# First self-attention by head pairs, its bias table turned once and added by VectorE

## The chip, the cores and the metric

One core of one Trainium2 chip runs the kernel. The time is what the device takes for one execution, in microseconds (us). The kernel before takes 2659.75 us, the median of three runs from 2657.06 to 2670.86. Everything is computed in float32. The engines are TensorE (PE in the profile, its weight loads PEld), VectorE (DVE), ScalarE (ACT), GpSimd (POOL) and SyncE (SP, which issues the DMAs of the weights).

## The reference, cut to what matters

A first block on 256 tokens of width 1024 (attention, then a mixture of 16 experts) is followed by blocks of a second model (latent attention, neighbourhood attention, two feed-forward stages). The change lies in the attention of the first block. Its scores have a bias that depends on the distance of key and query alone.

```python
def diff_attention(qa, ka, va, lam, lambda_init, subln_g, bias_a):     # 4 heads, two sides of 64 features each
    ...
    s1 = jnp.einsum('bhqd,bhkd->bhqk', q1, k1).astype(jnp.float32) + bias
    s2 = jnp.einsum('bhqd,bhkd->bhqk', q2, k2).astype(jnp.float32) + bias
    p = jax.nn.softmax(s1, axis=-1) - lam * jax.nn.softmax(s2, axis=-1)
    return jnp.einsum('bhqk,bhkd->bhqd', p.astype(v.dtype), v)
    ...
    o = rms_norm(o, subln_g, SUBLN_EPS) * (1.0 - lambda_init)
```

The dilated attention beside it has 8 heads of 64 features. Its three window patterns are joined into one softmax whose bias holds the logarithm of how many patterns allow a distance. The results of both, side by side (`mix`, 512 columns each), go through `w_out`.

## The kernel before

**Sizes.** 256 tokens are two halves (`NT` = 2) of 128 rows (`P`), 1024 features are eight blocks (`KC`) of 128. Weights stream through a ring of eight slots. SyncE issues the pieces in the order in which they are planned, each as soon as the piece eight before it has been used: `w_in` (8 pieces), `ada_w` (16), `w_out` (3), then the expert weights `w_gate`, `w_up` and `w_down` with the weights of the latent attention between them.

**Ahead of the attention.** `run_p` and `run_pv` (line 316) make queries and keys (`qkT`, features on the partitions) and values (`vv`, tokens on the partitions). The bias table goes through memory and comes back as `window`, 12 tables of 384 columns, one per head; a row of it stands in reversed order of the partitions, so that it has to be multiplied by `flip`, a reversed identity, before it is a bias.

**The attention** is 16 units: four differential heads with two sides each, then eight dilated heads. A unit has 256 queries against 256 keys, one PSUM bank of 512 columns. Class `Attention` (lines 386 to 516) is shared with the latent attentions of later stages. TensorE's order for unit u is: scores of u+1 (line 413), one piece of the `ada_w` product (line 744, eight matmuls of 384 columns into four groups of 32 output partitions), the four transposes of the probabilities of u (line 425), and the product with the values of u-1 (line 439). The scores (`unit1`, line 968) are for each token half a product of 64 rows, queries against keys, and on top of it a product of 128 rows, `flip` against `window`, which adds the bias. DVE takes the row maxima from PSUM (line 475), copies the transposed probabilities (line 502), takes the reciprocals of the sums (line 508), and puts the result into `mix`, scaled (line 491); the second side of a differential head is scaled by minus lambda as well and added to the first (line 489). ScalarE computes the exponentials (line 464) with the sums beside them.

**Behind the attention** the rows of the `ada_w` product leave PSUM (`row_out`, line 1124: rows 0 and 2 on ScalarE, 1 and 3 on DVE), are turned (`run_ada`), the differential half of `mix` is normed on DVE (lines 1222 to 1233), `run_m` turns all eight blocks of `mix` into `hT`, and `run_o` multiplies by `w_out`. Then come norm, router, expert choice (DVE) and the experts.

**Class `PairAttention`** (lines 519 to 630) does the neighbourhood attention near the end of the program, with 512 columns per side. It takes two heads of 64 features together, adds a bias table from SBUF on DVE, negates and takes the maximum in one instruction (line 612), norms the probabilities ahead of the transposes (line 620), turns them (line 558), and multiplies by the values in four groups of 32 output partitions (line 568), so that the result has the features on the partitions. Its tables are turned by `flip` beforehand (line 285, `na_window`).

## Time and profile before

| | us |
|---|---|
| median of three runs | 2659.75 |
| lowest and highest | 2657.06, 2670.86 |
| profiled execution, its own time | 2659.27 |
| its span in the trace | 2657.5 |
| TensorE busy | 2200.3 (83%) |
| DVE busy | 533.1 (20%) |
| ScalarE busy | 244.6 (9%) |

The mean granted clock of TensorE is 0.949 of full speed. The chain of work that ended last is PE for 58% of the span and DMA for 33%. For a change of one stage the shares of the whole span say little: what counts is which engine has no gap in the stage itself, and whether what follows starts when the stage ends or at a time of its own. The stage changed here runs from 112.40 to 200.18 us.

### The profile page before, as it was taken

How to read it: one execution, taken by the hardware profiler on the slowest of the kernel's cores; microseconds unless marked ns; L12 is line 12 of the kernel's file. 1: busy time of each engine (PE TensorE's matmuls, PEld its weight loads, DVE VectorE, ACT ScalarE, POOL GpSimd, SP SyncE). 2: the span in 40 equal slices, each digit the busy share in tenths (PEclk: the TensorE clock that was granted, in tenths of full speed). 3: DMA queues.
4: the chain of work that ended last, by engine and by line, in shares of the span. 5: the costliest groups of instructions: out<-in, count | busy, mean ns of one | idle time of the engine just before them, and what ended most of it. 6: DMA issues, size and time to landing. Idle time of an engine off the chain costs nothing.

```text
span 2657.5 us, 27028 instructions
## 1 busy us (share of the span) xinstructions
PE 2200.3 (83%) x11636; PEld 1134.9 (43%) x11636; DVE 533.1 (20%) x931; ACT 244.6 (9%) x550; POOL 30.0 (1%) x60
## 2 busy tenths in 40 slices
PE   6996978977687788778778655579989999989998
PEld 5553433432233333333333111146556656445665
DVE  0134111223101101110110311123310021063002
ACT  1121200100000000000000000011110020061000
POOL 0000000000000000000000000000000020000000
PEclk9998989989899899999989889989999999999999
DMA  7671599998999999999999999974094431124450
GB/s 269 251 284 69 223 424 409 425 390 362 425 416 420 419 418 417 420 420 412 420 416 405 424 425 425 423 313 179 16 320 147 153 134 64 64 78 134 152 158 32
DMA packets 146333, 781.00 MB, mean 294 GB/s; under 512 B 11156, under 2 KB 66171, under 8 KB 93491
## 3 DMA queue, kind: packets, MB, share of 16 engines
q1 hardware_dynamic: 139880, 769.45, 72.4%
q10 hardware_dynamic: 6346, 9.95, 1.2%
q8 instruction: 88, 1.44, 0.2%
q14 instruction: 19, 0.15, 0.0%
HBM read 778.29 MB, written 1.07 MB: 293 GB/s over the span
## 4 chain that ended last, share of the span: by engine, by line
PE 58%; DMA 33%; DVE 5%; issue 2%; ACT 1%; ACTq 0%; POOL 0%; SPq 0%; POOLq 0%; DVEq 0%
PE ps L285 15%; DMA ring<-in_mlp_w 12%; DMA ring<-in_w_down 10%; PE ps L1958 8%; PE ps L1965 8%; DMA ring<-in_w_gate 7%; PE ps L1721 4%; PE ps L413 4%; PE ps L1590 3%; PE ps L316 3%; PE ps L1562 3%; PE ps L1567 2%; PE ps L1601 2%; PE ps L439 1%; DMA ring<-in_w_up 1%
## 5 line engine op out<-in xcount | busy, mean ns | idle before, releaser
L1562 PE MATMUL ps<-ring,xe 128*32 128x512 f32 x2048 | 297.5, 648 | 138.7 <-DMA ring<-in_w_up 54.2
L1590 PE MATMUL ps<-ring,expert_work 128*32 128x512 f32 x1408 | 226.0, 703 | 31.4 <-DMA ring<-in_w_down 20.1
L1567 PE MATMUL ps<-ring,xe 128*32 128x256 f32 x2048 | 202.8, 464 | 0.0
L1562 PEld LDWEIGHTS ps<-ring,xe 128*32 128x32 f32 x2048 | 57.4, 113 | 256.4 <-issue 90.9
L1567 PEld LDWEIGHTS ps<-ring,xe 128*32 128x32 f32 x2048 | 73.1, 112 | 171.3 <-issue 171.3
L1590 PEld LDWEIGHTS ps<-ring,expert_work 128*32 128x32 f32 x1408 | 60.7, 123 | 188.6 <-issue 126.3
L1576 PE MATMUL ps<-cst,expert_work 128*128 128x128 f32 x96 | 24.9, 430 | 138.5 <-DVE expert_work L1624 138.5
L1721 PE MATMUL ps<-ring,h 128*128 128x512 f32 x256 | 114.1, 598 | 14.3 <-DMA ring<-in_mlp_w 14.3
L1713 PE MATMUL ps<-hT,ring 128*128 128x256 f32 x512 | 114.8, 382 | 11.6 <-DMA ring<-in_mlp_w 11.6
L1958 PE MATMUL ps<-mlp_x_hT,ring 128*128 128x256 f32 x512 | 114.3, 383 | 1.9 <-DVE mlp_x_hT L364 1.9
L1958 PE MATMUL ps<-mlp_n_hT,ring 128*128 128x256 f32 x512 | 112.6, 379 | 1.8 <-DVE mlp_n_hT L364 1.8
L1965 PE MATMUL ps<-ring,mlp_x_h 128*128 128x512 f32 x256 | 111.8, 592 | 0.0
L1965 PE MATMUL ps<-ring,mlp_n_h 128*128 128x512 f32 x256 | 111.8, 592 | 0.0
L1713 PEld LDWEIGHTS ps<-hT,ring 128*128 128x128 f32 x512 | 96.0, 190 | 33.7 <-DMA ring<-in_mlp_w 19.0
L1958 PEld LDWEIGHTS ps<-mlp_x_hT,ring 128*128 128x128 f32 x512 | 98.4, 192 | 20.5 <-issue 7.4
L1958 PEld LDWEIGHTS ps<-mlp_n_hT,ring 128*128 128x128 f32 x512 | 97.2, 190 | 19.9 <-issue 7.3
L285 PE MATMUL ps<-na_hT,ring 128*128 128x256 f32 (+1 forms) x256 | 82.8, 486 | 1.6 <-ACT na_hT L352 1.6
L1576 PEld LDWEIGHTS ps<-cst,expert_work 128*128 128x128 f32 x96 | 18.5, 221 | 148.3 <-DVE expert_work L1624 148.3
L1721 PEld LDWEIGHTS ps<-ring,h 128*128 128x128 f32 x256 | 47.3, 190 | 78.0 <-issue 78.0
L1618 DVE RECIPROCAL expert_work<-expert_work 128x768 f32<-128x768 f32 x16 | 79.2, 4953 | 0.6
L1810 DVE TENSOR_TENSOR h<-h 128x512 f32<-128x512 f32 x16 | 11.1, 692 | 332.7 <-ACT h L1779 332.7
L1616 DVE TENSOR_SCALAR expert_work<-expert_work 128x768 f32<-128x768 f32 x16 | 8.9, 559 | 318.8 <-ACT expert_work L1608 318.8
(376 smaller groups left out, 2137.6 us busy)
## 6 DMA issues: line engine op xcount, KB each, us to landing
ring<-in_w_gate SPq DMA_DIRECT2D x128, 1408.0 KB, 18.8
ring<-in_w_up SPq DMA_DIRECT2D x128, 1408.0 KB, 19.2
ring<-in_w_down SPq DMA_DIRECT2D x112, 1536.0 KB, 23.7
ring<-in_mlp_w SPq DMA_DIRECT2D x96, 1024.0 KB, 9.0
ring<-in_ada_w SPq DMA_DIRECT2D x32, 1536.0 KB, 9.1
ring<-in_w_in SPq DMA_DIRECT2D x8, 1536.0 KB, 21.8
ring<-in_na_w_qkv SPq DMA_DIRECT2D x12, 1024.0 KB, 9.0
ring<-in_w_down SPq DMA_DIRECT2D x16, 512.0 KB, 23.9
```

The costliest lines, as they stand in the source:

```text
L285: last = nc.tensor.matmul(bank[0:rows, lo:hi], lhsT, rhs, start=start, stop=stop)
L316: last = nc.tensor.matmul(self.part(i), lhsT, rhs, start=(k == 0 and i % self.per == 0), stop=(k == depth - 1), skip_group_check=True)
L413: last = nc.tensor.matmul(ps[:, self.bank + u % 2, lo:hi], lhsT, rhs, start=start, stop=stop, skip_group_check=True)
L1562: nc.tensor.matmul(ps[32 * j:32 * j + 32, up, :], xe[:, k, :], w[:, :, 4 * j:4 * j + 4], start=(k == 0), stop=(k == KC - 1))
L1567: last = nc.tensor.matmul(ps[32 * j:32 * j + 32, 2, 256 * up:256 * up + 256], xe[:, k, :], two, start=(k == 0 and not up), stop=(k == KC - ...
L1590: last = nc.tensor.matmul(ps[32 * j:32 * j + 32, 1 + half, :], hgT[:, at:at + 32], w[:, (c - c0) * D + 512 * half:(c - c0) * D + 512 * hal ...
L1601: last = nc.tensor.matmul(ps[:, 2 * t + half, :], gs[:, t * P:(t + 1) * P], ye[:, 512 * half:512 * half + 512], start=True, stop=True)
L1618: nc.vector.reciprocal(eg[:, 0:768], eg[:, 0:768]).then_inc(e_own, 1)
L1713: last = nc.tensor.matmul(ps[:, 3, S * fc:S * fc + S], w1[:, k, fc * P:(fc + 1) * P], buf["hT"][:, k, :], start=(k == 0), stop=(k == KC - 1))
L1721: last = nc.tensor.matmul(ps[:, CB[2 * t + half], :], m_h1[:, g, S * fc + t * P:S * fc + (t + 1) * P], w2[:, fc, 512 * half:512 * half + 512],
L1958: last = nc.tensor.matmul(ps[:, g % 2, S * fc:S * fc + S], w1[:, k, fc * P:(fc + 1) * P], hT[:, k, :], start=(k == 0), stop=(k == KC - 1))
L1965: last = nc.tensor.matmul(ps[:, 4 + 2 * t + half, :], h1[:, g, fc, t * P:(t + 1) * P], w2[:, fc, 512 * half:512 * half + 512], start=False ...
```

## The change

The first attention no longer uses `Attention` but a class of its own, `FirstAttention`, with eight units instead of 16: a unit is a differential head with both sides, or two dilated heads.

- `run_w1` turns the 12 tables ahead of the attention: 12 matmuls of `flip` against `window` (384 columns), whose results go back into `window`, on ScalarE and DVE in turn. The scores no longer hold a product with `flip`.
- The scores of a unit are four products of 64 rows and 256 columns, in banks 0 and 1, the sides on row halves 0 to 63 and 64 to 127 in turn. The scores of the next unit wait until DVE has taken those of this one (`top`).
- DVE adds the table, negates and takes the extremum in one instruction for each side and token half (256 columns), four to a unit. ScalarE's exponential then reads SBUF. DVE scales the probabilities by the reciprocals; the second side of a differential head is scaled by minus lambda and added to the first, so that one set of probabilities is left to be turned.
- A differential unit has four transposes, a dilated one eight (two sets). ScalarE copies them from PSUM (512 columns each); before, DVE did.
- The values of a differential unit are four products of 128 columns. Those of a dilated unit are eight products with 32 weight columns and 256 moving columns, in four groups of output partitions; their result is `hT` itself, so that `run_m` turns four blocks in place of eight.
- Two pieces of the `ada_w` product stand in each unit. All 16 use banks 6 and 7: after the eighth, ScalarE takes rows 0 and 1 out (`between`), and TensorE waits for that ahead of the ninth (`half0_out`). Rows 0 and 1 no longer leave PSUM behind the attention.
- `vrow`, `hot` and `plog` move into other buffers, and lambda into another column. Norms of the differential results are as before.

```diff
+                self.turns, n = [], 0
+                for unit in units:
+                    sides = range(1) if unit["lam"] is not None else range(2)
+                    self.turns.append([n + b for b in sides])
+                    n += len(sides)
...
+            def pe(self, pe):
+                def scores(u):
+                    if u >= 1:
+                        pe.wait_ge(self.top, 4 * u)
+                    q, k = self.units[u]["qk"]
+                    for t in range(NT):
+                        for b in range(2):
+                            rows = slice(HD * b, HD * b + HD)
+                            last = nc.tensor.matmul(ps[:, b, t * S:t * S + S], qkT[rows, q, t * P:(t + 1) * P], qkT[rows, k, :],
+                                                    start=True, stop=True, skip_group_check=True)
+                    last.then_inc(self.scored, 1)
+                def turn_over(u):
+                    for b, i in enumerate(self.turns[u]):
+                        pe.wait_ge(self.scaled, 4 * u + (4 if len(self.turns[u]) == 1 else 2 * b + 2))
+                        if i >= 2:
+                            pe.wait_ge(self.copied, i - 1)
+                        for c in range(2):
+                            for t in range(NT):
+                                at = t * S + c * P
+                                last = nc.tensor.transpose(ps[:, 2 + i % 2, (c * NT + t) * P:(c * NT + t) * P + P],
+                                                           self.probs[u % 3][:, b, at:at + P], ident)
+                        last.then_inc(self.turned, 1)
+                def times_values(u):
+                    pe.wait_ge(self.copied, self.turns[u][-1] + 1)
+                    if u >= 2:
+                        pe.wait_ge(self.out, u - 1)
+                    for out, lhsT, rhs, start, stop in self.units[u]["values"](ps[:, 4 + u % 2, 0:S], self.probsT[u % 2]):
+                        last = nc.tensor.matmul(out, lhsT, rhs, start=start, stop=stop, skip_group_check=True)
+                    last.then_inc(self.valued, 1)
+                n = len(self.units)
+                scores(0)
+                for u in range(n):
+                    self.fill(pe, 2 * u)
+                    if u >= 1:
+                        times_values(u - 1)
+                    if u + 1 < n:
+                        scores(u + 1)
+                    self.fill(pe, 2 * u + 1)
+                    turn_over(u)
+                times_values(n - 1)
...
+            def act(self, act, between):
+                n = len(self.units)
+                for u in range(n + 1):
+                    if u < n:
+                        for b in range(2):
+                            for t in range(NT):
+                                probs = self.probs[u % 3][:, b, t * S:t * S + S]
+                                act.wait_ge(self.top, 4 * u + 2 * b + t + 1)
+                                if u >= 3:
+                                    act.wait_ge(self.inverse, u - 2)
+                                nc.scalar.activation(probs, probs, ACT.Exp, bias=self.columns(0, u, 2 * b + t, 1), scale=-1.0,
+                                                     accum_out=self.columns(1, u, 2 * b + t, 1)).then_inc(self.exped, 1)
+                    if u >= 1:
+                        for b, i in enumerate(self.turns[u - 1]):
+                            act.wait_ge(self.turned, i + 1)
+                            if u >= 3:
+                                act.wait_ge(self.valued, u - 2)
+                            nc.scalar.activation(self.probsT[(u - 1) % 2][:, b, :, :].rearrange("p c q -> p (c q)"),
+                                                 ps[:, 2 + i % 2, :], ACT.Identity).then_inc(self.copied, 1)
+                    between(act, u)
...
+            def dve(self, dve):
+                n = len(self.units)
+                for u in range(n + 1):
+                    if u >= 2:
+                        self.result(dve, u - 2)
+                    if u == n:
+                        continue
+                    unit = self.units[u]
+                    dve.wait_ge(self.scored, u + 1)
+                    if u >= 3:
+                        dve.wait_ge(self.turned, self.turns[u - 3][-1] + 1)
+                    for b in range(2):
+                        for t in range(NT):
+                            nc.vector.tensor_tensor_reduce(self.probs[u % 3][:, b, t * S:t * S + S], ps[:, b, t * S:t * S + S],
+                                                           unit["table"](b, t), -1.0, 0.0, ALU.add, ALU.min,
+                                                           self.columns(0, u, 2 * b + t, 1)).then_inc(self.top, 1)
+                    dve.wait_ge(self.exped, 4 * u + 4)
+                    nc.vector.reciprocal(self.columns(2, u), self.columns(1, u)).then_inc(self.inverse, 1)
+                    dve.wait_ge(self.inverse, u + 1)
+                    if unit["lam"] is not None:
+                        second = self.columns(2, u, 2, 2)
+                        link(dve, nc.vector.tensor_scalar(second, second, unit["lam"], None, ALU.mult))
+                    for b in range(2):
+                        for t in range(NT):
+                            part = self.probs[u % 3][:, b, t * S:t * S + S]
+                            inv = self.columns(2, u, 2 * b + t, 1)
+                            if b and unit["lam"] is not None:
+                                whole = self.probs[u % 3][:, 0, t * S:t * S + S]
+                                dve.wait_ge(self.scaled, 4 * u + t + 1)
+                                last = nc.vector.scalar_tensor_tensor(whole, part, inv, whole, ALU.mult, ALU.add)
+                            else:
+                                last = nc.vector.tensor_scalar(part, part, inv, None, ALU.mult)
+                            last.then_inc(self.scaled, 1)
+                self.result(dve, n - 1)
+            def result(self, dve, u):
+                dve.wait_ge(self.valued, u + 1)
+                self.units[u]["evac"](ps[:, 4 + u % 2, 0:S]).then_inc(self.out, 1)
...
-        def unit1(q, k, hh, table, v, out, minus=None):
-            lo = HD * (hh % 2)
-            sc = []
-            for t in range(NT):
-                sc.append((t * S, t * S + S, qkT[lo:lo + HD, q, t * P:(t + 1) * P], qkT[lo:lo + HD, k, :], True, False))
-                off = P * (1 - t)
-                sc.append((t * S, t * S + S, flip, window[:, table, off:off + S], False, True))
-            return {"nt": NT, "scores": sc, "v": v, "out": out, "minus": minus}
...
+        for hh in range(DIFF_HEADS + DIL_HEADS // 2):
+            diff = hh < DIFF_HEADS
+            qk = (hh, 4 + hh) if diff else (8 + hh - DIFF_HEADS, 12 + hh - DIFF_HEADS)
+            def table(b, t, hh=hh, diff=diff):
+                n = hh if diff else DIFF_HEADS + 2 * (hh - DIFF_HEADS) + b
+                return window[:, n, P * (1 - t):P * (1 - t) + S]
+            def values(bank, turned, hh=hh, diff=diff):
+                if diff:
+                    return [(bank[:, t * P:t * P + P], turned[:, 0, c, t * P:t * P + P], vv[:, c, P * hh:P * hh + P], c == 0, c == 1)
+                            for t in range(NT) for c in range(2)]
+                return [(bank[32 * n:32 * n + 32, :], vv[:, c, P * hh + 32 * n:P * hh + 32 * n + 32], turned[:, n // 2, c, :],
+                         c == 0, c == 1) for c in range(2) for n in range(4)]
+            def evac(bank, hh=hh, diff=diff):
+                if diff:
+                    return nc.vector.tensor_copy(mix[:, :, P * hh:P * hh + P], bank.rearrange("p (t f) -> p t f", t=NT))
+                return nc.vector.tensor_copy(hT[:, hh, :], bank)
+            units.append({"qk": qk, "lam": small[:, 60:61] if diff else None, "table": table, "values": values, "evac": evac})
...
-        att1 = Attention("a1", units, probs, probsT, fill=lambda pe, u: ada_piece(pe, 0, u, ada_base, 4 + 2 * (u // KC)))
+        rows0 = view(vac, 4, ADA_W)
+        def row_out(row, bank, eng):
+            src = ps[:, bank, 0:ADA_W]
+            return nc.scalar.activation(row, src, ACT.Identity) if eng == "act" else nc.vector.tensor_copy(row, src)
+        def fill(pe, i):
+            if i == KC:
+                pe.wait_ge(half0_out, 1)
+            ada_piece(pe, 0, i, ada_base, 6)
+        def between(act, u):
+            if u == KC // 2:
+                act.wait_ge(ada_done.sem, ada_base + KC)
+                row_out(rows0[:, 0, :], 6, "act")
+                row_out(rows0[:, 1, :], 7, "act").then_inc(half0_out, 1)
...
+        run_w1 = Run([Job([((P, 0, WIN), flip, window[:, n, :], True, True, False, None)],
+                          *turn(n, window[:, n, :], cols=WIN)) for n in range(12)], (2, 3, 4, 5))
+        att1 = FirstAttention(units, probs1, probsT1, fill)
         @block.tensor
         def _(pe):
...
             run_pv.finished(pe)
+            run_w1.pe(pe)
+            run_w1.finished(pe)
             att1.pe(pe)
...
-            att1.act(act)
+            run_w1.ev(act, "act")
+            att1.act(act, between)
         @block.vector
         def _(dve):
-            att1.dve(dve, dve_own, dve_count)
+            run_w1.ev(dve, "dve")
+            run_w1.finished(dve)
+            att1.dve(dve)
...
-        run_m = Run(transposes(KC, lambda t, c: mix[:, t, c * P:(c + 1) * P], lambda c: hT[:, c, :],
+        run_m = Run(transposes(DIFF_HEADS, lambda t, c: mix[:, t, c * P:(c + 1) * P], lambda c: hT[:, c, :],
...
-            row_out(rows0[:, 0, :], 4, "act").then_inc(a2.sem, a2("row0"))
...
-            row_out(rows0[:, 1, :], 5, "dve").then_inc(v2.sem, v2("row1"))
...
```

On TensorE, in the attention, a unit stood like this before; it is one side of a differential head (`ps<-qkT` and `ps<-window,cst` are scores, these two rows stand twice, `ps<-ring,scp` is the `ada_w` piece, `ps<-cst,probs` the transposes, `ps<-vv,probsT` the values):

```order
L413 MATMUL ps<-qkT 128x256 [waits exp_done]
L413 MATMUL ps<-window,cst 128x256
...
L744 MATMUL ps<-ring,scp 32x384 [waits slot1_loaded]
L744 MATMUL ps<-ring,scp 32x384 x7
L425 MATMUL ps<-cst,probs 128x128 [waits probT_sb,exp_done]
L425 MATMUL ps<-cst,probs 128x128 x3
L439 MATMUL ps<-vv,probsT 128x128 [waits probT_sb]
L439 MATMUL ps<-vv,probsT 128x128 x3
```

Now a unit is the whole head (this is the third of four); `kTc` and `table_parts` are further buffers of the probabilities and of their transposes:

```order
L871 MATMUL ps<-ring,scp 32x384 [waits slot4_loaded]
L871 MATMUL ps<-ring,scp 32x384 x7
L681 MATMUL ps<-vv,table_parts 128x128 [waits a1_copied]
L681 MATMUL ps<-vv,table_parts 128x128 x3
L660 MATMUL ps<-qkT 128x256 [waits a1_top]
L660 MATMUL ps<-qkT 128x256 x3
L871 MATMUL ps<-ring,scp 32x384 [waits slot5_loaded]
L871 MATMUL ps<-ring,scp 32x384 x7
L672 MATMUL ps<-cst,kTc 128x128 [waits a1_copied,a1_scaled]
L672 MATMUL ps<-cst,kTc 128x128 x3
```

For a head, eight products of scores have become four, eight transposes four, and eight value products four; the two pieces are still two.

On ScalarE, at the end of the attention before, the first rows of the `ada_w` product (`vac`) came last, behind all exponentials:

```order
L464 ACTIVATE probs,small<-ps,small 128x256 [waits out_done,probT_done,max_done]
L464 ACTIVATE probs,small<-ps,small 128x256
L1197 UNCONDITIONAL_BRANCH
L1124 ACTIVATE vac<-ps 128x384 [waits ada_done]
L1124 ACTIVATE vac<-ps 128x384
L1203 ACT_TABLE_LOAD
```

Now rows 0 and 1 stand in the middle of it, between the copies of the transposes of two units:

```order
L706 ACTIVATE kTc,small<-kTc,small 128x256 [waits a1_inverse,a1_top] x4
L713 ACTIVATE table_parts<-ps 128x512 [waits a1_valued,a1_turned]
L1126 ACTIVATE vac<-ps 128x384 [waits ada_done]
L1126 ACTIVATE vac<-ps 128x384
L706 ACTIVATE kTc,small<-kTc,small 128x256 [waits a1_inverse,a1_top] x4
L713 ACTIVATE probsT<-ps 128x512 [waits a1_valued,a1_turned] x2
```

The `vac` rows have moved up, behind the exponentials of the fifth unit and the copy of the fourth, and TensorE's ninth piece waits for them.

## Rows read from the trace of the kernel before

**Rows 1.** Timeline, PE, one unit: start us, us, engine line op tiles xcount [idle].
```profile
124.82 0.70 PE L413 MATMUL ps<-qkT 64*128 64x256 f32 x2
...
127.33 1.50 PE L744 MATMUL ps<-ring,scp 128*32 128x384 f32 x16
128.76 0.66 PE L425 MATMUL ps<-cst,probs 128*128 128x128 f32 x4
129.25 1.06 PE L439 MATMUL ps<-vv,probsT 128*128 128x128 f32 x8
130.24 0.70 PE L413 MATMUL ps<-qkT 64*128 64x256 f32 x2
```

**Rows 2.** Busy time by stretch: PE, PEld, DVE, ACT, POOL; granted clock, DMA share, GB/s.
```profile
108.00:112.00 4.00, 3.52 (x9) 1.26 (x7) 1.13 (x2) 1.20 (x2) 0.00 (x0) 1.00 1.02 433
...
112.40:200.20 87.80, 86.53 (x576) 47.36 (x576) 32.85 (x84) 18.50 (x67) 0.00 (x0) 1.00 0.83 301
200.00:204.00 4.00, 2.55 (x12) 2.42 (x12) 3.80 (x8) 0.07 (x1) 0.00 (x0) 0.62 0.49 210
...
250.00:286.00 36.00, 20.93 (x72) 11.31 (x72) 18.29 (x36) 5.92 (x13) 0.00 (x0) 0.73 0.00 0
...
2320.00:2360.00 40.00, 36.22 (x230) 17.51 (x228) 24.89 (x78) 20.21 (x49) 0.00 (x0) 1.00 0.32 105
```

**Rows 3.** Timeline, PE and DVE, the attention's ends and what follows.
```profile
112.40 0.67 PE L413 MATMUL ps<-qkT 64*128 64x256 f32 x2 [0.88 <-DVE vv L359]
...
199.70 0.48 DVE L491 TENSOR_SCALAR h<-ps,small 128x64 f32<-128x64 f32 x2 [1.26 <-PE ps L439]
200.28 1.02 DVE L1124 COPY vac<-ps 128x384 f32<-128x384 f32 x2
...
206.11 2.18 PE L283 MATMUL ps<-cst,h 128*128 128x128 f32 x16 [1.87 <-DVE modc L761]
...
208.91 27.70 PE L285 MATMUL ps<-ring,hT 128*128 128x512 f32 x64 [0.62 <-ACT hT L352]
```

**Rows 4.** Timeline, PE, the turning of the tables of the neighbourhood attention.
```profile
2173.77 5.34 PE L285 MATMUL ps<-na_window,cst 128*128 128x384 f32 x16
```

**Rows 5.** Timeline, PE, the neighbourhood attention; and line 316's products of 256 columns.
```profile
2342.51 1.05 PE L568 MATMUL ps<-na_hT,na_v 128*32 128x256 f32 x16
2343.49 1.13 PE L547 MATMUL ps<-na_kT,kTc 64*128 64x512 f32 x4
2344.55 1.09 PE L558 MATMUL ps<-cst,na_window 128*128 128x128 f32 x8
...
28.57 55.49 PE L316 MATMUL ps<-hT,ring 128*128 128x256 f32 x256 [0.98 <-DVE plog L829]
```

**Rows 6.** Timeline, DVE, the neighbourhood attention: one unit, 512 columns a side.
```profile
2345.28 0.69 DVE L612 CUSTOM_DVE_ANT_1 na_window<-ps,ring 128x512 f32<-128x512 f32 x1
...
2346.25 0.17 DVE L618 RECIPROCAL small<-small 128x1 f32<-128x1 f32 x1 [0.27 <-ACT na_window L599]
2346.45 0.49 DVE L620 TENSOR_SCALAR na_window<-na_window,small 128x512 f32<-128x512 f32 x1
...
2350.43 0.42 DVE L2293 COPY kTc<-ps 128x256 f32<-128x256 f32 x1
```

**Rows 7.** Timeline, ACT: exponential of 256 columns, row outs, exponential of 512, copies.
```profile
115.71 0.47 ACT L464 ACTIVATE probs<-ps,small 128x256 f32<-128x256 f32 x1 [4.41 <-DVE small L475]
...
196.50 0.87 ACT L1124 ACTIVATE vac<-ps 128x384 f32<-128x384 f32 x2 [2.56 <-PE ps L744]
...
2345.40 0.72 ACT L599 ACTIVATE na_window<-na_window,small 128x512 f32<-128x512 f32 x1 [1.29 <-DVE small L612]
...
2346.82 1.06 ACT L589 ACTIVATE na_hT<-ps 128x512 f32<-128x512 f32 x2
```

**Rows 8.** SyncE's first issue after the attention (timeline); an `ada_w` piece, median us to landing.
```profile
236.65 0.93 SPq L243 DMA_DIRECT2D ring<-in_mla_w_dq  x2
...
ring<-in_ada_w SPq DMA_DIRECT2D x16, 1536.0 KB, 7.6
```

42 lines of the change are left out of this document (22 added, 20 removed).

## Prediction

> **What bounds the kernel now.** I read four views, in this order. The busy time by stretch comes first [rows 2]: in the attention, 112.40 to 200.20 us, TensorE is busy for 86.53 of 87.80 us, at full clock, while DVE has 32.85 and ScalarE 18.50. So the stage costs what TensorE's instructions cost, and only what leaves TensorE there shortens it. The timeline of one unit [rows 1] says what they are: from 124.82 to 130.24 are 5.42 us, of which the scores take 2.51, the `ada_w` piece 1.43, the transposes 0.49 and the values 0.99. 16 units make the stage. The third view is what follows it [rows 3]: the last result leaves DVE at 200.18, and the output projection starts at 208.91. Between them runs one chain on DVE with two bursts of transposes. The fourth is whether the rest waits for this stage or for the memory. SyncE's first issue after the stage is at 236.65 [rows 8], and the DMA share is 0.00 from 250 to 286 [rows 2]: the ring is full and the expert stage starts when its inputs are computed. So a microsecond won in the attention should be a microsecond at the end, although the experts themselves are fed at DMA pace.
>
> **What TensorE pays in the new stage.**
> Turning the tables: eight matmuls of 384 columns took 5.34 us elsewhere [rows 4], about 0.65 each with the overlaps. 12 x 0.65 = 7.8, and 0.6 for the last result to leave PSUM, with nothing beside it on TensorE. From 112.40 that gives 120.8 for the first scores.
> Scores: four products of 256 columns, alternating between the row halves. The pair of 512 columns in the neighbourhood attention starts 1.06 us before the next work [rows 5], where one after the other they would need 4 x 0.43 = 1.7 (55.49 us for 256 instructions, two to a product, is 0.43 for 256 columns [rows 5]). It has the same number of column passes as ours, so 1.06. Bounds: 1.06 and 1.7. 8 x 1.06 = 8.5.
> Pieces: 16 x 1.43 = 22.9, as before.
> Transposes: four sets of 0.49 for the differential heads and eight for the dilated ones, 12 x 0.50 = 6.0.
> Values: a differential unit has the four products that a unit had before, 0.99. A dilated one has eight products in four column groups; the same eight took 0.98 in the neighbourhood attention (2342.51 to 2343.49 [rows 5]), against 8 x 0.43 = 3.4 if they don't overlap. 4 x 0.99 + 4 x 0.95 = 7.8.
> Sum: 8.5 + 22.9 + 6.0 + 7.8 = 45.2 us, or 5.4 for a differential unit and 5.9 for a dilated one.
>
> The Trainium skill, "TensorEngine Tiling (Array Packing)", section Key Properties, says that a change of tiling mode drains TensorE. The trace agrees for the old scores, where 64 rows and 128 rows alternate: 2.51 / 4 = 0.63 for each product [rows 1] against 0.43 where nothing alternates [rows 5]. Read strictly it charges a differential unit one change more than I count, some 0.2, which would make the sum 1.6 worse.
>
> **What DVE and ScalarE pay for a unit.** From the scores on: the first table addition is 256 columns, 0.69 for 512 [rows 6] less the 0.27 by which the 256-column copy (0.42) is shorter, so 0.42. Then four exponentials, 0.47 from PSUM at 256 columns and 0.72 from SBUF at 512 [rows 7]; I take 0.50 each, 2.0. The other three additions hide under them. Then a reciprocal 0.17, the lambda step with its link some 0.27, and four scalings of 256 columns, 0.49 for 512 [rows 6], so 0.28 to 0.42 each, 1.4 together. With the result copy of 0.42 and semaphores that is 4.8 us per unit, against 5.4 to 5.9 on TensorE. ScalarE has 2.0 and one or two copies of 0.53 [rows 7], 3.1 at most. TensorE therefore stays the bound by about 0.6, a thin margin at the start of the stage and in the differential half.
>
> **Waits of TensorE in the new stage.** I followed the queues by these numbers. (1) The start: the first unit has no unit before it whose values could fill the time. The scores of unit 1 wait 0.2 for the additions of unit 0, its transposes 0.5 for the scalings (ready at 126.4), and its values 1.1, because ScalarE's copy stands behind the exponentials of unit 1. After that TensorE is late enough for the others. (2) The ninth piece: ScalarE must finish the exponentials of unit 4, the copy of unit 3 (0.53) and two rows (0.87 [rows 7]). Behind the transposes of unit 3 this makes 2.1; with the exponentials done it would be 1.5. Queued behind it on TensorE are the values of unit 3 and the scores of unit 5. (3) The end: the last values wait 0.75 for the last copy, which no other work covers. Together 1.8 + 2.1 + 0.75 = 4.6 us. Bounds: 2.5 (the start covered, the ninth piece at 1.5) and 8 (0.4 more in each unit).
>
> End of TensorE's part: 120.8 + 45.2 + 4.6 = 170.6; the last copy by DVE ends at 171.0. Before it was 200.18: **29.2 us less**.
>
> **Behind the stage.** Row 1 no longer leaves PSUM on DVE's chain: half of 1.02 [rows 3], 0.5. `run_m` turns four blocks, not eight: half of 2.18 and of the copies that trail it, 1.0 of the 2.80 between 206.11 and 208.91 [rows 3]. ScalarE's row and its table load fit under DVE's squares as before. 1.5 us less.
>
> **Transfers.** At full backlog the DMAs move 433 GB/s [rows 2], 3.6 us for a piece of 1.57 MB. The new stage uses a piece every 2.8 us, but starts with eight in the ring. The ninth is issued when the first is used, at about 123.3, and lands after 7.6 [rows 8], the sixteenth some 7 x 3.66 later, at 156 to 157. It is wanted at about 166. `w_out` follows until about 167, wanted at 178. Covered at no cost; the cover is some 10 us wide.
>
> **Sum.** 29.2 + 1.5 = 30.7 us. The profiled execution took 2659.27, half a microsecond off the median of 2659.75, so 2659.3 - 30.7 = 2628.6; with a small part of the mode changes, **2629**.
>
> **Rivals.**
> (A) *DVE and ScalarE set the pace.* For it: 4.8 against 5.4 is little, every unit has a ring of semaphores through three engines, and no row shows these instructions at 256 columns. If the additions are 0.45, the exponentials 0.60, the scalings 0.40 to 0.50, a unit comes to 5.6 to 5.8 and the stage to 175.0, 2633. If all cost as much as at 512 columns, some 7.5 a unit, 8 x 7.5 = 60: 2644. Against it: the fixed part of each row is small beside its columns. The Trainium skill warns of this in "TensorEngine Tiling (Array Packing)", section PSUM Bottleneck: tiling speeds TensorE but not the evacuation of PSUM, which may become the bottleneck.
> (B) *The small products don't overlap.* Scores 1.7 (+5.1 for eight units) and dilated values 3.4 (+9.9): 2644. Against it stand the 1.06 and 0.98 of the same forms [rows 5].
> (C) *Transfers.* If pieces come no faster than at the pace of 301 GB/s of the old stage [rows 2], 5.2 us each, the sixteenth lands near 168 and `w_out` near 182: +4, 2633. Against it: 433 GB/s in the backlog.
> (D) *Slower than before: the clock.* The granted clock was 0.62 from 200 to 204 [rows 2], behind waits. The new stage has more waits. If TensorE ran at 1.2 instead of 2.4 GHz through it, 45.2 + 7.8 us would double: +53, 2682. It turns slower than before from 31 us, that is 60% of the stage at the low level. Against it: the neighbourhood attention has waits in each unit, 36.22 us busy of 40, and kept 1.00 [rows 2].
> (E) *Nothing arrives at the end.* The stage is shorter, but the experts wait for weights whose transfer ends no earlier: 2659. It decides if their first five pieces land later than the router is done. They are issued from about 157 on and need some 17 us; the experts start near 256.
>
> **How the numbers follow.** Forecast (2625 to 2632) 0.67; A 0.14, B 0.06, C 0.04, D 0.03, E 0.03, and 0.03 for more gain, should the waits vanish. The range is the forecast with its bounds, C and the lighter part of A: 2624 to 2636, 0.8 or a little more. A gain of over 0.5% (13 us, about what a measurement can tell from none) holds in all but D and E: faster 0.94, same 0.03, slower 0.03.
>
> **What would show it.** Right: first scores at 120.8, eight units of 5.4 to 5.9 in TensorE's timeline, one wait of about 2 us ahead of the ninth piece, the last result near 171, the projection near 178, and the expert stage 30 to 31 us earlier, with equal gaps from there on. Wrong: waits of TensorE for DVE's scalings in every unit (A), scores of 1.7 or values of 3.4 (B), waits for `ada_w` or `w_out` (C), a granted clock under 1.00 between 121 and 170 (D), experts that start earlier and then wait longer for the ring (E).

## The result, and the profile after

The changed kernel takes **2630.07 us**, the median of four executions from 2628.27 to 2637.34. The kernel before, run beside it, takes 2662.91 (four executions, 2657.06 to 2670.86). The ratio is 0.9885, with a 95% interval from 0.9864 to 0.9906: faster, by 25 to 36 us. Forecast were 2629 and a gain of 30.7 us, which is a ratio of 0.9885 as well.

The profiled execution is the longest of the four: 2637.34, a span of 2635.5. It is 21.9 us below the profiled execution of before, not 30.7. Most of this text is about the 9 us between these two numbers.

The page of after, busy time of each engine (us, share of the span, instructions):

```profile
PE 2174.7 (83%) x11540; PEld 1120.3 (43%) x11540; DVE 530.0 (20%) x966; ACT 252.8 (10%) x567; POOL 29.9 (1%) x60
```

TensorE has 96 instructions less and is busy for 25.6 us less than before (2200.3 in the table ahead); DVE is about where it was. Now the stage itself, TensorE's timeline (start, us from first to last, engine, line, operation, output and inputs, count; in brackets the idle time ahead of the row and what ended it):

```profile
116.09 7.98 PE L285 MATMUL ps<-window,cst 128*128 128x384 f32 x24 [0.88 <-DVE vv L359]
124.81 1.14 PE L660 MATMUL ps<-qkT 64*128 64x256 f32 x8 [0.74 <-DVE window L359]
...
127.66 1.13 PE L660 MATMUL ps<-qkT 64*128 64x256 f32 x8 [0.28 <-DVE small L730]
...
130.65 0.66 PE L672 MATMUL ps<-cst,probs 128*128 128x128 f32 x4 [0.43 <-DVE probs L746]
...
133.58 1.16 PE L681 MATMUL ps<-vv,probsT 128*128 128x128 f32 x8 [0.85 <-ACT probsT L713]
134.67 1.13 PE L660 MATMUL ps<-qkT 64*128 64x256 f32 x8
...
137.16 0.66 PE L672 MATMUL ps<-cst,kTc 128*128 128x128 f32 x4
137.75 1.50 PE L871 MATMUL ps<-ring,scp 128*32 128x384 f32 x16
139.18 1.16 PE L681 MATMUL ps<-vv,table_parts 128*128 128x128 f32 x8
140.26 1.13 PE L660 MATMUL ps<-qkT 64*128 64x256 f32 x8
...
150.86 2.29 PE L871 MATMUL ps<-ring,scp 128*32 128x384 f32 x16 [1.86 <-ACT vac L1126]
153.08 1.98 PE L681 MATMUL ps<-vv,table_parts 128*128 128x128 f32 x8
154.99 1.13 PE L660 MATMUL ps<-qkT 64*128 64x256 f32 x8
...
158.51 1.50 PE L871 MATMUL ps<-ring,scp 128*32 128x384 f32 x16
159.82 1.05 PE L681 MATMUL ps<-probsT,vv 128*32 128x256 f32 x16
160.80 1.14 PE L660 MATMUL ps<-qkT 64*128 64x256 f32 x8
...
175.53 1.07 PE L681 MATMUL ps<-table_parts,vv 128*32 128x256 f32 x16 [0.74 <-ACT table_parts L713]
177.90 1.50 PE L283 MATMUL ps<-cst,vac 128*128 128x128 f32 x12 [1.30 <-DVE vac L1126]
182.57 1.97 PE L283 MATMUL ps<-cst,h 128*128 128x128 f32 x8 [3.16 <-DVE modc L888]
185.16 29.59 PE L285 MATMUL ps<-ring,hT 128*128 128x512 f32 x64 [0.62 <-ACT hT L352]
```

These rows answer to those of [rows 1] and [rows 3]. From one scores row to the next, 134.67 to 140.26, a differential unit takes 5.59 us, for two sides; [rows 1] had 5.42 for one. A dilated unit takes 5.81, 154.99 to 160.80, for two heads. The brackets are all the waits of the stage: 0.74, 0.28, 0.43 and 0.85 at the start, 1.86 ahead of the ninth piece, 0.74 at the end. All other rows of the stage follow each other without one. The stage ends with the last result's copy at 176.67 + 0.42 = 177.09, so it takes 61.00 us from 116.09, against 87.78 before.

Three of these rows are longer than their neighbours of the same form: the ninth piece has 2.29 where 1.50 is usual, the values behind it 1.98 for 1.16, and the output projection 29.59, where before had 27.70. The stretches of after show TensorE's granted clock there (length; then busy us and instructions of PE, PEld, DVE, ACT and POOL; granted clock, DMA share, GB/s):

```profile
121.00:145.00 24.00, 21.70 (x184) 10.69 (x183) 14.56 (x59) 11.10 (x38) 0.00 (x0) 1.00 0.80 326
152.00:154.00 2.00, 2.00 (x12) 0.92 (x5) 0.00 (x0) 0.00 (x0) 0.00 (x0) 0.50 0.98 418
...
182.00:184.50 2.50, 1.93 (x8) 1.57 (x8) 1.35 (x8) 0.82 (x2) 0.00 (x0) 0.53 1.00 424
184.50:188.00 3.50, 2.88 (x5) 1.32 (x5) 0.48 (x1) 0.12 (x1) 0.00 (x0) 0.50 0.50 207
```

The clock is full (2.4 GHz) until the wait of 1.86, at 1.2 GHz behind it, and again at 1.2 GHz behind the wait of 3.16. Between the two, `run_ada` (177.90) takes 1.50 at full clock. In the profile of before it took nearly twice as long, in the stretch from 200 to 204 us whose granted clock was 0.62 [rows 2]:

```profile
201.45 2.79 PE L283 MATMUL ps<-cst,vac 128*128 128x128 f32 x12 [1.79 <-DVE vac L1124]
```

A third place at a lower pace lies ahead of the change. The first projections (line 316), which no edit touches, took 58.53 us in the profile of after and 55.49 in that of before [rows 5]. TensorE's timeline of after:

```profile
29.23 58.53 PE L316 MATMUL ps<-hT,ring 128*128 128x256 f32 x256 [0.98 <-DVE table_parts L959]
```

Six microseconds of it, columns as in the stretches above:

```profile
29.00:35.00 6.00, 5.77 (x14) 4.64 (x15) 0.00 (x0) 0.00 (x0) 0.00 (x0) 1.00 1.02 421
```

The same six of `e_side_order`, an experiment that differs from after only in the attention:

```profile
29.00:35.00 6.00, 6.00 (x29) 5.30 (x28) 0.00 (x0) 0.00 (x0) 0.00 (x0) 1.00 1.02 425
```

Of the same matmuls 14 fit in where 29 do in the other: half the pace. The column of the granted clock reads 1.00 in both, so here the pace has to be read from the instructions. The matmul ahead of them (line 285, at 26.37) took 1.88 against 1.08 as well. This is why the stage begins at 116.09 and not at 112.40.

**The account of the 8.8 us**, profile against profile (forecast 30.7, seen 21.9):

| | forecast | profile of after | missing |
|---|---|---|---|
| start of the stage | 112.40 | 116.09 | 3.7 |
| stage | 87.8 - 29.2 = 58.6 | 61.0 | 2.4 |
| last result to projection | 7.2 | 185.16 - 177.09 = 8.07 | 0.8 |
| projection | 27.70 | 29.59 | 1.9 |

Of the 2.4 in the stage, 0.8 + 0.8 are the two long rows at 1.2 GHz. Of the 0.8 behind it, all is `run_m`, whose eight transposes took 1.97 where 1.09 is usual. With the start and the projection that makes 8.0 us of half-pace stretches; the other 0.8 us are true errors of the sum, told below.

### The profile page after: what moved, and what is told of

The parts are those of the page before. It is cut to its first block, busy times and chain, and to the rows that moved or that the text cites. A ratio compares the mean times of both kernels' runs of the same rounds, so it can differ in the third digit from the quotient of the medians.

```text
span 2635.5 us, 26842 instructions
## 1 busy us (share of the span) xinstructions
PE 2174.7 (83%) x11540; PEld 1120.3 (43%) x11540; DVE 530.0 (20%) x966; ACT 252.8 (10%) x567; POOL 29.9 (1%) x60
## 4 chain that ended last, share of the span: by engine, by line
PE 59%; DMA 31%; DVE 5%; issue 2%; ACT 2%; SPq 1%; ACTq 0%; POOL 0%; POOLq 0%; DVEq 0%
PE ps L285 16%; DMA ring<-in_mlp_w 10%; DMA ring<-in_w_down 10%; PE ps L2109 8%; PE ps L2116 8%; DMA ring<-in_w_gate 7%; PE ps L1741 4%; PE ps L1872 4%; PE ps L1713 3%; PE ps L316 3%; PE ps L413 2%; PE ps L1718 2%; PE ps L1752 2%; SPq L218 1%; DVE expert_work L1769 1%
## 5 line engine op out<-in xcount | busy, mean ns | idle before, releaser
L1741 PE MATMUL ps<-ring,expert_work 128*32 128x512 f32 x1408 | 225.5, 707 | 30.6 <-DMA ring<-in_w_down 19.4
L1961 DVE TENSOR_TENSOR h<-h 128x512 f32<-128x512 f32 x16 | 11.1, 692 | 332.6 <-ACT h L1930 332.6
## 6 DMA issues: line engine op xcount, KB each, us to landing
ring<-in_w_in SPq DMA_DIRECT2D x8, 1536.0 KB, 21.9
```

The costliest lines, as they stand in the source:

```text
L1741: last = nc.tensor.matmul(ps[32 * j:32 * j + 32, 1 + half, :], hgT[:, at:at + 32], w[:, (c - c0) * D + 512 * half:(c - c0) * D + 512 * hal ...
```

## The experiments

All times "of the stage" are from TensorE's first work after the value projection to the end of the last result's copy. A single execution is uncertain by some 5 us (the four of after span 9), so where a part is judged I read the stage and give the total beside it; the total of a single execution can't resolve a part smaller than that.

### Both kernels again

The changed kernel and the one before, unchanged, to see which of the slow stretches belong to the kernel.

> The changed kernel once more. Theory 1 (the 7 us by which its profiled execution is longer than its other runs are stretches at 1.2 GHz that fall elsewhere in each execution): the profile is 3 to 8 us shorter than 2637.34, the queries and keys projections take 55.5 us in place of 58.5 unless a low stretch falls on them again, and the stage from the first table product to the last result is again 59 to 61 us. Theory 2 (they belong to the new kernel): the same three places (first projection, ninth piece, output projection) are at the low clock again, and the time is 2637.

Median 2630.35 (2625.44 to 2636.44, four executions) against 2659.99 (seven), ratio 0.9885 (0.9859 to 0.9911). TensorE's timeline:

```profile
28.93 58.13 PE L316 MATMUL ps<-hT,ring 128*128 128x256 f32 x256 [0.98 <-DVE table_parts L959]
...
150.17 2.69 PE L871 MATMUL ps<-ring,scp 128*32 128x384 f32 x16 [1.86 <-ACT vac L1126]
...
184.48 29.39 PE L285 MATMUL ps<-ring,hT 128*128 128x512 f32 x64 [0.62 <-ACT hT L352]
```

All the long rows are back, the ninth piece behind the same wait, and the stage is 61.0 us again. One thing differs: here `run_ada` is at the low clock already (2.42 for 1.50), and the wait behind it is 2.24, not 3.16.

> The kernel before once more, for its profile. If the low clock in the output projection belongs to the new kernel, the projection takes 27.7 us again. If it is chance, it takes 29 or more here in one case of two. The 512-column stretch of the queries and keys at the start takes 55.5 or 58 to 58.6 us by chance, as in the others.

2665.74 us. This profile of the old kernel has fast first projections (55.49) but a slow output projection:

```profile
205.94 3.67 PE L283 MATMUL ps<-cst,h 128*128 128x128 f32 x16 [1.87 <-DVE modc L761]
210.24 29.53 PE L285 MATMUL ps<-ring,hT 128*128 128x512 f32 x64 [0.62 <-ACT hT L352]
```

So 29.53 is possible for the old kernel too. My theory that the low clock of the projection belongs to the new kernel alone falls. Over all profiles, those of the new form without filled gaps had 29.3 to 30.6 in nine of nine, those of the old form 27.70, 27.70 and 29.53 (the second is `e_before_no_table`, below). But the granted clock fell to 0.50 behind the stage in all three of the old form as well; what differs is which rows it fell on. In before these were `run_ada`'s alone, in `e_before_no_table` `run_ada` and `run_m` (2.01 and 3.41), in `e_before_again` all three.

The low clock at the ninth piece does not come with every execution. Of eight profiles with a wait of 1.86 to 1.90 ahead of it, only after and `e_after_again` have a long ninth piece; in the other six it takes 1.50. Nor do the slow first projections follow from the change: over 14 profiles they are there in seven (56.9 to 58.6 us), in kernels of both forms, and no edit but that of the table's store reaches ahead of them.

### What the bias product costs

In the kernel before, the product of `flip` and `window` is taken out of the scores. This leaves the bias out.

```
-                sc.append((..., qkT[lo:lo + HD, q, ...], qkT[lo:lo + HD, k, :], True, False))
-                sc.append((..., flip, window[:, table, off:off + S], False, True))
+                sc.append((..., qkT[lo:lo + HD, q, ...], qkT[lo:lo + HD, k, :], True, True))
```

> The kernel before without the products of the table, so the bias is left out of the first attention. Theory (TensorE bounds the old stage by the sum of its instructions, and 64-row and 128-row products in turn cost 0.63 each where they need 0.43): scores go from 2.51 to about 1.06 us a unit, a unit from 5.42 to about 4.0, the stage from 87.8 to about 65 us. If the table product only costs its own 0.43 and hides nothing else, 1.65 us remain for the scores and the stage is 74. Rival (the old stage is bound by the ring of waits through DVE and ScalarE): it stays over 80.

2644.08 us, and the stage falls from 87.8 to 64.0. TensorE's timeline:

```profile
123.41 1.13 PE L413 MATMUL ps<-qkT 64*128 64x256 f32 x4
124.47 1.50 PE L744 MATMUL ps<-ring,scp 128*32 128x384 f32 x16
...
127.37 1.13 PE L413 MATMUL ps<-qkT 64*128 64x256 f32 x4
```

A unit takes 3.96 (123.41 to 127.37; its neighbours 3.97), not 5.42; the scores start 1.06 before the next work, not 2.51. So the two bias products and the changes between 64 and 128 rows cost 1.45 us of each of 16 units, 23 us together, most of what the change wins. The rest of the change, turning the tables included, brings the stage from 64.0 to 59.4 (the next run). A second thing stands in these rows: x4 is two products, both on one half of the rows, and they take the same 1.06 as the four products over both halves in the new kernel. Twice 0.43, the price of a product of 128 rows and 256 columns [rows 5], leaves 0.2 for the changes of form on either side; the other half's products come on top at no cost.

### The order of the row halves

The forecast took 1.06 for the scores because the halves alternate.

```
-                    for t in range(NT):
-                        for b in range(2):
+                    for b in range(2):
+                        for t in range(NT):
```

> The changed kernel with one edit: the four score products of a unit run side by side no longer alternate between the row halves, both products of one half come first. Theory (products on the two halves run at the same time only when they alternate): scores go from 1.06 to 1.3 to 1.7 us a unit, the stage gets 2 to 5 us longer. Rival (each product costs its columns anyway and the saving in the scores is only the missing change of mode): scores stay at 1.06, the stage is the same within 0.5 us.

2631.82 us. TensorE's timeline:

```profile
130.68 1.14 PE L660 MATMUL ps<-qkT 64*128 64x256 f32 x8
131.75 1.50 PE L871 MATMUL ps<-ring,scp 128*32 128x384 f32 x16
...
146.90 1.50 PE L871 MATMUL ps<-ring,scp 128*32 128x384 f32 x16 [1.87 <-ACT vac L1126]
```

Still 1.06, with both products of one half issued ahead of the other's. My reason was wrong, the number right: the halves run side by side, but they needn't alternate for it. This run is also a clean view of the stage. The wait of 1.87 is there and no low clock behind it; the stage takes 112.10 to 171.53, **59.4 us** against 58.6 forecast (`e_gap_filled`, below, has 59.4 too). Its projection still has 29.57.

### How far DVE is from being the bound (rival A)

Copies of 256 columns are added on DVE in each unit, between the reciprocal and the scalings.

```
+                    for _ in range(2):          # the other run: range(6)
+                        link(dve, nc.vector.tensor_copy(extra[:, :], window[:, 0, 0:S]))
```

> The changed kernel with two extra copies of 256 columns on DVE in each unit, between the reciprocals and the scalings, some 0.8 to 1.0 us a unit on the path to the transposes. Theory (TensorE sets the pace and DVE has 0.65 us to spare in a unit): the stage gets 2 to 4 us longer, most of it at the start and in the differential units. Rival A (DVE and ScalarE set the pace already): 8 units by 0.9, 7 us longer or more.

2633.02 us. TensorE's timeline of it:

```profile
130.87 0.66 PE L672 MATMUL ps<-cst,probs 128*128 128x128 f32 x4 [1.08 <-DVE probs L748]
```

DVE's timeline of it, in a differential unit:

```profile
138.87 0.62 DVE L737 COPY extra<-window 128x256 f32<-128x256 f32 x2
...
141.11 0.42 DVE L1120 COPY h<-ps 128x256 f32<-128x256 f32 x1
141.66 0.42 DVE L730 CUSTOM_DVE_ANT_0 probs<-ps,window 128x256 f32<-128x256 f32 x1
```

The two copies add 0.65 us to each unit, less than I had expected, and DVE has almost no gap left: its first addition follows the result copy by 0.13. In DVE's timeline of after the same place has a gap of 0.65:

```profile
140.37 0.42 DVE L1117 COPY h<-ps 128x256 f32<-128x256 f32 x1
141.44 0.43 DVE L730 CUSTOM_DVE_ANT_0 probs<-ps,window 128x256 f32<-128x256 f32 x1 [0.65 <-PE ps L660]
```

TensorE's units stay at 5.59 and 5.81; only the start shows it, where the wait for the scalings grows from 0.43 to 1.08. The stage is 60.0 us, 0.6 more than 59.4, where I had expected 2 to 4.

> The changed kernel with six extra copies on DVE in each unit; two cost DVE 0.65 us, so six cost 1.95. Theory (DVE had 0.65 us to spare in a differential unit of 5.59 and about 1.2 in a dilated one of 5.81): differential units get 1.3 us longer, dilated ones 0.8, the start 1.9; the stage goes from 59.4 to 67 to 70 us. If DVE's true margin is larger, because its wait for ScalarE's exponentials can take some of it, 63 to 65.

2639.48 us. Six copies, 1.95 us, break it: the stage is 67.05, 7.6 more than 59.4. Up to 3.2 us of that are low clock, in two places (2.79 for a piece and 0.97 for the transposes ahead of it at the start, 2.45 and 1.84 for the ninth piece and the values behind it). The rest are waits: 2.40 for the scalings at the start, 0.32 and 1.00 for ScalarE's copy in the next units, which take 5.98 and 6.67, and 3.18 ahead of the ninth piece. TensorE:

```profile
152.43 2.45 PE L873 MATMUL ps<-ring,scp 128*32 128x384 f32 x16 [3.18 <-ACT vac L1129]
```

0.65 us in a unit is hidden and 1.95 is not. That the margin is about what the forecast said (0.6) rests on DVE's gap of 0.65; these two runs only bracket it. Without the low clock the stage would take 63.9 to 65.4 us (an estimate: 67.05 less 3.2, or less the 1.6 at the ninth piece alone), less than the 67 to 70 of the theory.

### The two sides turned apart

The second side of a differential head isn't added to the first; both are turned and multiplied.

```
-                    sides = range(1) if unit["lam"] is not None else range(2)
+                    sides = range(2)
...
-                            if b and unit["lam"] is not None:
-                                ...
-                                last = nc.vector.scalar_tensor_tensor(whole, part, inv, whole, ALU.mult, ALU.add)
-                            else:
-                                last = nc.vector.tensor_scalar(part, part, inv, None, ALU.mult)
+                            last = nc.vector.tensor_scalar(part, part, inv, None, ALU.mult)
...
-                    return [(bank[...], turned[:, 0, c, ...], vv[...], c == 0, c == 1) for t ... for c ...]
+                    return [(bank[...], turned[:, b, c, ...], vv[...], b + c == 0, b + c == 2) for t ... for b ... for c ...]
```

> The changed kernel with the two sides of a differential head turned and multiplied apart, added up in PSUM. Theory (TensorE bound): four more transposes (0.5) and four more value products (1.0) in each of four units, the stage 6 us longer. Rival: TensorE had idle time there, and 3 us or less are lost.

2635.38 us, the stage 64.5, 5.1 more. TensorE:

```profile
136.64 2.05 PE L681 MATMUL ps<-vv,table_parts 128*128 128x128 f32 x16
...
143.56 2.05 PE L681 MATMUL ps<-vv,probsT 128*128 128x128 f32 x16
```

A differential unit takes 6.92 (136.64 to 143.56), not 5.59. Joining the sets is worth 1.33 in each of four units.

### The ninth piece behind the values

The piece that waits for the first two rows of `ada_w` is moved behind the values of unit 3 and the scores of unit 5.

```
-                    self.fill(pe, 2 * u)
+                    if u != n // 2:
+                        self.fill(pe, 2 * u)
...
+                    if u == n // 2:
+                        self.fill(pe, 2 * u)
```

> The changed kernel with the ninth piece of the modulation product behind the values of unit 3 and the scores of unit 5 instead of ahead of them. Theory: the wait of 1.86 us ahead of it goes, and the low clock that followed it in the profile (the piece 2.2 in place of 1.43 us, the values 1.9 in place of 1.1) goes too; the stage is 1.5 to 3.5 us shorter. Rival: the values of unit 3 wait for the same ScalarE queue, and 1 us or less is left of the gain.

2632.67 us, the stage 58.5. That is 0.9 less than 59.4, the rival's figure. It is 2.5 less than the 61.0 of after, but the low clock in that is absent from most profiles anyway. TensorE:

```profile
146.30 1.16 PE L681 MATMUL ps<-vv,table_parts 128*128 128x128 f32 x8 [1.11 <-ACT table_parts L716]
```

The wait of 1.86 becomes one of 1.11, for ScalarE's copy of the transposed set, which the next work needs. ScalarE's queue is what is late here, not the piece.

### The table read in its own order

The turning of the tables is 8.7 us in which TensorE does nothing else. It is needed because a row of `window` starts one element further for each partition. If the store writes a copy of each table for each partition (128 rows of 512 elements per head), a read that steps 511 elements from the last element of the first row delivers the other order, and neither `flip` nor `run_w1` is needed.

```
-        table_dram = nc.dram_tensor("bias_table", [12, 512], F32).ap()
+        table_dram = nc.dram_tensor("bias_table", [12, P, 512], F32).ap()
...
-            sp.dma_start(table_dram, plog[0:12, :])
-            src = bass.AP(..., offset=table_dram.offset, ap=[[1, P], [512, 12], [1, WIN]])
+            sp.dma_start(table_dram, plog[0:12, :]....to_broadcast([12, P, 512]))
+            src = bass.AP(..., offset=table_dram.offset + P - 1, ap=[[511, P], [P * 512, 12], [1, WIN]])
...
-            run_w1.pe(pe)
...
-            run_w1.ev(act, "act")
-            run_w1.ev(dve, "dve")
+            dve.wait_ge(win_loaded, 16)
```

> The changed kernel with the tables turned by the memory instead of TensorE: the table is stored 128 times in a row, and read with a step of 511 from one partition to the next, so that it arrives turned. The 12 table products and their copies are gone. Theory: the first scores start where the first table product started, 8.7 us earlier, and all of it arrives at the end: 8 to 9 us less than the changed kernel. Rival: the larger store and its reading (3 MB each way) run beside the loads of the first weights and hold up the projections or arrive after 112 us: the same time or longer.

**2619.0 us** (2618.77 to 2621.03, four executions) against 2663.81 (seven), ratio 0.9837 (0.982 to 0.9853), an interval clear of the changed kernel's. It beats both kernels. TensorE's timeline:

```profile
112.40 1.14 PE L660 MATMUL ps<-qkT 64*128 64x256 f32 x8 [0.87 <-DVE vv L359]
...
170.25 29.40 PE L285 MATMUL ps<-ring,hT 128*128 128x512 f32 x64 [0.65 <-ACT hT L352]
```

SyncE's queue (start, us to issue):

```profile
28.33 0.97 SPq L1018 DMA_DIRECT2D bias_table<-table_parts  x1
81.25 0.39 SPq L1021 DMA_DIRECT2D window<-bias_table  x1
```

The scores start when the values are ready, and the stage takes 50.6 us, 8.8 less than 59.4, as the turning with its wait had cost. The median is 11.1 us below the changed kernel's; the further 2.3 are within the interval's width. The price is a slow store: 3.1 MB, and SyncE can issue the read that waits for it only at 81.25, not at 42.07 as in after. It is in time: the read lands 9.3 us after its issue and is wanted at 112.40, and the next piece of `ada_w` is issued at 87.52, in after at 91.22. A stretch of the store:

```profile
60.00:70.00 10.00, 10.00 (x48) 8.81 (x47) 0.00 (x0) 0.00 (x0) 0.00 (x0) 1.00 0.71 76
```

76 GB/s at a DMA share of 0.71, with nothing else under way (in after the share is 0.00 from 60 to 81); a backlog of weights has 1.00. The Trainium skill, "DMA: Bandwidth & Descriptors", section Rules for kernel authors, says that a transfer whose outermost dimension has fewer than 16 entries is confined to at most as many engines. The outermost here has 12, and by that page a share of 12 / 16 = 0.75 is my estimate; the row's 0.71 agrees. A store cut otherwise wasn't tried.

### Both, and the gap behind the stage filled

`e_both` is the direct table with the ninth piece moved.

> Turned by the memory and the ninth piece later, together. Theory: the gains add, 10 to 12 us less than the changed kernel, near 2619. Rival: the pieces of the modulation weights or the output weights now arrive late, since TensorE asks for them earlier while the DMAs already run at their full rate through the second half of the stage: 5 us or less of gain and waits for the ring.

Median 2621.64 (2617.89 to 2627.08), stage 49.8: 0.8 us less in the stage than `e_direct_table`, and nothing that the totals resolve: 8.4 us less than the changed kernel, not 10 to 12. Its first projections were slow (58.05).

In the next two, 20 transposes whose results nobody reads stand in TensorE's wait for DVE behind `run_ada`, in the changed kernel and in the one with the direct table.

```
             run_ada.pe(pe)
+            for _ in range(20):
+                nc.tensor.transpose(ps[:, 4, 0:P], ident, ident)
```

> The changed kernel with 20 spare transposes (2.8 us of TensorE, into a bank that is free) behind the turning of the modulation rows, where TensorE otherwise idles 3.16 us. Theory (the idle time puts the clock to 1.2 GHz just ahead of the output projection, which so far took 29.4 to 30.6 us in every profile of the new family and 27.70 in both of the old one): the projection takes 27.7 to 28.3, and the time is 1 to 2.5 us less than the changed kernel's 2630. Rival (where the clock falls is chance, or spare transposes don't keep it up): 29 to 31 us again, the same time.

TensorE of `e_gap_filled`:

```profile
176.12 2.35 PE L1330 MATMUL ps<-cst 128*128 128x128 f32 x20
179.45 1.09 PE L283 MATMUL ps<-cst,h 128*128 128x128 f32 x8 [0.98 <-DVE modc L888]
181.19 27.70 PE L285 MATMUL ps<-ring,hT 128*128 128x512 f32 x64 [0.65 <-ACT hT L352]
```

The wait of 3.16 is down to 0.98, `run_m` has 1.09, the projection 27.70 and starts 7.23 after the last result, exactly the forecast's 7.2. But the median is 2629.47 (2626.95 to 2634.42), beside 2630.07 and 2630.35 of the unfilled kernel: a local gain of 2.7 us that the totals don't show.

> The tables turned by the memory, and the spare transposes in the gap. Theory: the two gains add, 1 to 2.5 us less than the 2619.0 of the table turned by the memory alone. Rival as for the gap filled alone: 2619.

Projection 27.70 again, median 2620.99 (2612.49 to 2626.11) beside 2619.0: the executions lie further apart, and again the totals don't tell.

## Why the prediction was right

The sum stands at nearly every term. At full clock, from the rows above:

- **Turning the tables**: 8.72 us from 116.09 to 124.81; forecast 8.4. The products took 7.98, as 5.34 / 8 [rows 4] gives for twelve; the sum had 7.8. The last result's way out of PSUM was 0.74, not 0.6.
- **Scores** 1.06, **pieces** 1.43, **dilated values** 0.98 (159.82 to 160.80), each as forecast. Only the piece ahead of the dilated values, in tiles of the same form (128*32), is shorter: 1.31 (158.51 to 159.82). That the scores need alternating halves was a wrong reason for a right number (`e_side_order`).
- **Differential unit** 5.59 for 5.4, **dilated unit** 5.81 (154.99 to 160.80) for 5.9. The mis-sized terms are the values of a differential unit, 1.08 (139.18 to 140.26) against the 0.99 taken over from [rows 1], and the transposes, 0.59 (137.16 to 137.75), not 0.50. In [rows 1] these two followed each other in the same form of tile (128*128); now a piece (128*32) stands between them. This is the 0.2 of a further mode change that the forecast set beside its sum; the sum had priced it at nothing. The Trainium skill, "TensorEngine Tiling (Array Packing)", section Key Properties, says that changing the tiling mode drains TensorE. These rows agree with it: a change costs 0.09 to 0.12 us, the 1.31 included, which has one change less than the 1.43.
- **Waits**: start 0.28 + 0.43 + 0.85 = 1.56 for 1.8, ninth piece 1.86 for 2.1, end 0.74 for 0.75. The reason for the ninth piece, ScalarE's queue, stands in ScalarE's timeline of after, and `e_ninth_later` confirms it: the two rows end at 149.96 + 0.84 = 150.80, and the piece starts at 150.86.

```profile
149.49 0.57 ACT L713 ACTIVATE table_parts<-ps 128x512 f32<-128x512 f32 x1
149.96 0.84 ACT L1126 ACTIVATE vac<-ps 128x384 f32<-128x384 f32 x2
```

- **Together** the stage is 59.4 us where no low clock fell into it, forecast 58.6.
- **Behind the stage**: 7.23 us with the gap filled, forecast 7.2, but 8.07 in the kernel as it is. Here a step failed: the forecast took the durations of `run_m` and of the projection from before and didn't ask at which clock they would run. DVE's chain sets when `run_m` starts: 4.67 us after the start of `run_ada` in after (177.90 to 182.57), 4.66 in before (201.45 to 206.11 [rows 3]). So TensorE's wait is what `run_ada` leaves of that, 3.16 behind 1.50 us and 1.87 behind 2.79. In before the low clock fell on `run_ada` and cost nothing there. In after `run_ada` ran at full clock, and the low clock came behind the wait, on `run_m` and the projection, which nothing hides. The granted clock was 0.50 on one or both of these for some microseconds in nine profiles of nine, against 1.00 throughout in the two with the gap filled. From the last result to the end of the projection after takes 37.7 us, with the gap filled it is 34.9: 2.7 of the 30.7 are lost here. Over the nine profiles the loss is 1.6 to 3.0. The old form pays as well in some executions: it took 36.4 in before, 37.7 in `e_before_no_table` and 39.8 in `e_before_again`, so how much of the loss is the change's own stays open.

**The rivals.** A: DVE has 0.65 us to spare in a differential unit, so its part with its waits for ScalarE is 5.59 - 0.65 = 4.94 for the 4.8 forecast, and it was not the bound; 0.65 more is hidden, 1.95 is not. B: the small products do overlap. C: no row of TensorE waits for the ring; the pieces came at 419 GB/s from 148 to 186. D came true in small, and not in each execution: in two profiles of eight some 3 us of the stage ran at 1.2 GHz behind the longest wait. E: the experts start at 264.74, 22.0 earlier than before's 286.78, and from there to the end it is 2370.8 us, before 2370.7. What the stage gains arrives.

**The median and the profile.** The profile of after holds 8.0 us of half-pace stretches that the forecast did not foresee; before's own, on `run_ada`, cost it nothing. That the median still meets the forecast has two parts. Not every execution has them all (the first projections are slow in half of the profiles), and the profiled one was the longest of the four. And the median of before came out at 2662.9, 3.2 above the 2659.75 from which I worked, so that the medians lie 32.8 us apart. The part from the experts to the end, which no kernel here changes, took between 2364 and 2375 us. This scatter is larger than the low clock's local price, so how much of the total the low clock costs on average stays open. The terms of the sum are borne out row by row; that the medians meet the forecast to 1 us is in part luck.

## What to carry to other kernels

When an engine bounds a stage without a gap, a forecast row by row holds to a percent or two: take each form's pitch (start to start) from a place where the same form runs, and follow the queues through the first unit and each hand-over, since the waits lie there. Then look at what stands behind the stage: a stretch at low clock that another engine's chain hid before can fall on rows that nothing hides, and cost more than a term of the sum. And a product that only turns or adds a table is worth asking about twice: whether another engine can add it, and whether the memory can deliver it in the order in which it is used.

## What was unexpected of the hardware

- Executions of one kernel lie up to 14 us apart (before), 9 and 11 (after), and part of it has places: the first projections take 55.49 or 56.9 to 58.6, the output projection 27.70 or 29.3 to 30.6, the ninth piece 1.50 or 2.29 to 2.69. Behind the same wait of 1.86 to 1.90 the ninth piece was long in two profiles and at full pace in six. What decides it in an execution wasn't found.
- At 29 to 35 us TensorE ran at half pace while the granted clock read 1.00; the count of instructions in a stretch shows it.
- Behind the stage the granted clock fell to 0.50 in all twelve profiles in which the gap was not filled, old form and new, on different rows. Transposes that nobody reads, 2.35 us of them in a gap of 3.16, kept the following 1.09 and 27.70 at full pace, in two profiles of two.
- Two products of 64 rows on one half of TensorE take as long as four over both halves, 1.06 us, in whichever order the four are issued.
- A store of 3.1 MB whose outermost dimension is 12 moved 76 GB/s at a DMA share of 0.71.
